# Mixer's end in a two-layer decoder trunk: one softmax scaling moved ahead of a recurrence level, and the first output product's parts taken in another order

## The chip, the core and the metric

One NeuronCore of a Trainium2 chip runs the whole step as one program. The engines have queues of their own and meet at semaphores: TensorE (PE; PEld is its weight load), VectorE (DVE), ScalarE (ACT), GpSimd (POOL), and SyncE (SP), which here only issues DMAs. The metric is the device time of one execution, in microseconds (us); smaller is better.

## The reference, cut to what matters

Two layers of a hybrid decoder run over 256 prompt tokens and 8 x 4 sampled tokens (288 columns, features on the 128 partitions). Only the mixer's end, where three branches meet in one output projection, is touched:

```python
def mixer_layer(x, pos, attn, hg_state, conv_prev, g, w_in_l, w_out_l, lb, norm_g, cw):
    h = rmsnorm(x, g) @ w_in_l
    ...
    a = attn(q, k, v)                                   # 512 features: softmax attention
    o_h, S = hgrn2_mixer(hq, hf, hi, hg, lb, norm_g, hg_state)   # 256: gated recurrence
    yc, conv_new = causal_dwconv(cc * ch, conv_prev, cw)
    o_c = cb * yc                                       # 256: gated convolution
    y = jnp.concatenate([a, o_h, o_c.astype(a.dtype)], axis=-1) @ w_out_l
    return x + y, k, v, S, conv_new
```

The recurrence's output is normalised per head (`rmsnorm(o, norm_g)`) and gated before it enters the product. After the mixer come a cross-attention over 256 memory tokens (memory keys and values of the prompt are computed, those of the samples are read from a cache), and a gated MLP.

## The kernel before, in words

`layer_schedule` (L142) writes one order of steps per layer by hand. Each step has a name, arguments and a letter: "A" or "D" says that PE fills a bank of PSUM for it and that ACT or DVE empties the bank; "op" is a step without a bank, of the engines that handle its name. Every engine walks the same list and does its own part of each step, so the list sets the order on PE, ACT, DVE and POOL at once. Banks are used in turn, eight of them.

The steps that matter, with the lines of the profile:

- `as`, `anorm`, `at`, `ao` of g = 0 to 3 (attention of the prompt): DVE subtracts the maximum, ACT takes the exponential (L1077, L1079), `anorm` scales the probabilities on DVE (L1932 to L1936), PE transposes them (`at`, L1451), ACT copies, PE multiplies by the values (`ao`, L1457 to L1461).
- `level(m)`: one level of the recurrence. PE (L1527) fills two banks, DVE places them with a mask (L1976), and `merge` (DVE, L1996 to L1998) scales for the next level. m = 64 is the last; `cross` (L1539) follows.
- `ss`, `st`, `so`, `sot`: attention of the samples (`so` is L1483 and L1486 on PE, its ACT part is L1103, `sot` is L1497 on PE).
- `mk`, `mv`: keys and values of the prompt's memory (L1409, L1417 on PE), each emptied by one ACT copy (L964). On POOL the step `mv` 1 (L856) waits for ACT's copy, stores mv to memory (issue at L813), and then builds a table `vexp` (L864).
- `ho` 0 and 1 (PE L1561 to L1571; DVE L2017, L2019): output of the recurrence, two heads in each half. `hn` 0 and 1: sum of squares over a head (PE L1574), ACT's guess of the root (L976, a function with a table of its own), three DVE operations that refine it (L1759 to L1764) and two that apply it (L2026, L2029). DVE takes half 0 wholly before half 1.
- `split_mixed` k: tile k of the eight input tiles of the output projection is split in a rounded high part (ACT, L1123) and the rest (DVE, L2034). Tiles 0 to 3 are attention, 4 and 5 the recurrence's halves, 6 and 7 the convolution. `MIXED_ORDER` (L78) is the order in which PE takes them in the first output block.
- `round` / `rest` "out" m: the same split of the weights of output block m (ACT L1168, DVE L1822). SP loads block m's weights when PE has finished with the buffer: blocks 2 and 3 when `mv` 1 is done on PE, block 4 when block 0 is, and so on.
- `out` m (PE L1288 to L1290, 24 matmuls a block), m = 0 to 7. After each of the first six stands `turn_cmem` m: PE transposes (L1427) a cached memory-key block that POOL has loaded into `rawk`, which has two halves. On POOL the step `turn_cmem` b issues the load of cached block b + 2 (L798, through `load_rawk(l, b + 10)`) and then one of values (L878). `turn_cmem` 2 on PE thus needs the load that POOL issues in its step `turn_cmem` 0, which stands behind `mv` 1 and the store of `hstate` in POOL's order:

```python
                elif step == "turn_cmem":
                    b = args[0]
                    if b < 6:
                        load_rawk(l, b + 10)
```

After the change `mv` 1 stands behind all of the second group of `split_mixed` and behind `round` "out" 1 in the list; PE's own order from `sot` to `out` 0 is `sot`, `mv` 0, `mv` 1, `hstate`, `out` 0 in both kernels.

Of the kernel before, what the change touches and what calls it, by code (L numbers as in the profile page):

```python
# [29 lines left out]
ACT = mybir.ActivationFunctionType  # L30
# [44 lines left out]
    return (n + 3) % SLOTS  # L75


MIXED_ORDER = [6, 7, 4, 5, 0, 1, 2, 3]  # L78
DOWN_K = [(0, 8), (8, 16), (16, 22)]


# [55 lines left out]
def par_col(r, l, k=0):  # L137

    return r[0] + l * r[1] + k


def layer_schedule(l):  # L142
# [5 lines left out]
    def a(who, step, *args):  # L148
        s.append((step, args, who))

    def level(m):
        a("D", "level", m, 0)
        a("D", "level", m, 1)
        a("op", "merge", m)
# [9 lines left out]
    def project(part, m):  # L164

        p = 2 * [c[0] for c in IN_CHUNKS].index(part) + m
        if 4 <= p + 2 < IN_PIECES:
            a("op", "rest", "in", p + 2, l)
        a("D", "in", part, m)
        if p == (2 if first else 1):  # L170
            a("D", "ssq", 0)
        if 4 <= p + 3 < IN_PIECES:
            a("op", "round", "in", p + 3, l)
# [96 lines left out]
    scores(3)  # L270
    project("hg", 1)
    a("A", "ao", 2)
    level(64)
    a("op", "anorm", 3)
    a("A", "ss", 0)
    turn_probs(3)
    a("A", "ss", 1)
# [9 lines left out]
        a("A", "turn_ke", t)  # L287
    a("A", "st", 1)
    a("op", "conv")
    a("A", "mk", 1)  # L290
    a("A", "so", 0)
    a("D", "ho", 0)
    a("D", "ho", 1)
    a("A", "so", 1)
    a("D", "hn", 0)
    a("D", "hn", 1)
    a("A", "sot")
    a("A", "mv", 0)
    for k in (6, 7, 4, 5):
        a("op", "split_mixed", k)  # L300
    a("A", "mv", 1)
    a("op", "round", "out", 0, l)
    a("op", "rest", "out", 0, l)
    for k in (0, 1, 2, 3):
        a("op", "split_mixed", k)
    a("op", "round", "out", 1, l)
    a("op", "rest", "out", 1, l)
    a("A", "hstate")
    for m in range(8):
# [109 lines left out]
class Banks:  # L419


    def __init__(self):
        self.steps = [(-1, *x) for x in PROLOGUE]
        for l in range(DEPTH):
            self.steps += [(l, *x) for x in layer_schedule(l)]
        self.steps += [(DEPTH, *x) for x in EPILOGUE]
        self.emptying_steps = emptied_order(self.steps)
        fills = [x for x in self.steps if x[3] != "op"]
        self.of = {x[:3]: n for n, x in enumerate(fills)}
        emptied = {}  # L430
        for who, steps in (("A", self.steps), ("D", self.emptying_steps)):
            own = [x for x in steps if x[3] == who]
            emptied.update({x[:3]: (who, n + 1) for n, x in enumerate(own)})
        self.before = [emptied[x[:3]] for x in fills]


def decoder_kernel(nc, a, out):
# [4 lines left out]
    with ExitStack() as ctx:  # L442
        def sb(name, *shape, dt=F32):
            return ctx.enter_context(nc.sbuf_tensor(name, list(shape), dt))
# [27 lines left out]
        mv = sb("mv", P, 2, 256)  # L472
# [4 lines left out]
        small = sb("small", P, 112)  # L477
# [109 lines left out]
        eps = small[:, 56:57]  # L587
# [74 lines left out]
        def wait_emptied(eng, l, step, *args):  # L662

            who, count = banks.before[banks.of[l, step, args]]
            eng.wait_ge(emptied[who], count)
# [285 lines left out]
        def _(act):  # L951
            ac = nc.scalar.activation
# [26 lines left out]
            def gained(l, stage, k):  # L979

                if stage == 3:
                    wait_emptied(act, l, "down", k)
                elif l == 0 and stage == 0:
                    wait_emptied(act, -1, "turn_x", k)
                else:
                    before = (l, "out") if stage else (l - 1, "down")
                    wait_emptied(act, *before, k)
                c = R_FINAL + k if stage == 3 else par_col((R_MIX, R_XATTN)[stage], l, k)
                if stage or l:
                    ac(XG[:, k], X[:, k], ACT.Identity, scale=par[:, c:c + 1]).then_inc(s["xg_tile"], 1)  # L990
                if stage == 0:
                    ac(xg_hi_mix[:, k], X[:, k], ACT.Identity, scale=par[:, c:c + 1]).then_inc(s["xg_hi"], 1)

            for l, step, args, who in banks.emptying_steps:
                if step == "turn_x" and who == "A":
                    take(l, step, args, X[:, args[0]], bank(l, step, *args)[:, 0:N]).then_inc(emptied["A"], 1)
                elif step == "hi_x":
                    if args[0] == 0:
                        wait_emptied(act, l, "par_mix")
                    gained(0, 0, args[0])  # L1000
                elif step == "root_first":
                    act.wait_ge(s["eps"], 1)
                    ac(small[:, 48:49], eps, ACT.Abs_reciprocal_sqrt)
# [111 lines left out]
                elif step == "split_mixed":  # L1115
                    k = args[0]
# [33 lines left out]
                elif step == "round":  # L1150
                    kind, i, l = args
# [101 lines left out]
        def _(pe):  # L1253
# [15 lines left out]
            def parts_of(l, kind, i):  # L1269

                count, _, lo, hi_part, width, _ = split_of(kind, i, l)
                pe.wait_ge(w_lo_dve, count)
                if kind in ("up", "down"):
                    pe.wait_ge(w_lo_pool, count - SPLIT_PIECES * (l + 1))
                return [w.rearrange("p (k c) -> p k c", c=width) for w in (hi_part, lo)]
# [39 lines left out]
            for l, step, args, who in banks.steps:  # L1315
# [259 lines left out]
                elif step == "out":  # L1575
                    m = args[0]
                    hi_w, lo_w = parts_of(l, "out", m)
                    for n, k in enumerate(MIXED_ORDER):
                        if m == 0:
# [101 lines left out]
        def _(dve):  # L1681
# [93 lines left out]
            for l, step, args, who in banks.emptying_steps:  # L1775
# [255 lines left out]
                elif step == "split_mixed":  # L2031
                    k = args[0]
                    dve.wait_ge(s["mixed_hi"], 8 * l + MIXED_ORDER.index(k) + 1)
                    v.tensor_tensor(mixed_lo[k], mixed[k], mixed_hi[:, k].bitcast(F32), ALU.subtract).then_inc(s["mixed_lo"], 1)  # L2034
# [100 lines left out]
```

## Time and profile before

| | |
|---|---|
| median of 3 runs | 882.81 us (879.73 to 885.25) |
| the profiled execution's own time | 884.58 us |
| its span, first to last instruction | 882.9 us (1.7 us lie outside) |
| PE busy | 840.1 us, 95% |
| DVE / ACT / POOL busy | 65% / 52% / 42% |
| mean granted clock of PE | 0.978 |

The mixer's end is at 121 to 191 us in the first layer and at 545 to 616 us in the second. A timeline row reads: start, duration, engine, line, operation, output <- input, partitions x elements, count, and in brackets how long the engine sat idle before it and what ended that.

### The profile page before, as it was taken

To read this page: it belongs to the slowest core of one execution; us is meant where nothing else is said; L and a number is where in the kernel's file an instruction comes from. 1 tells how busy PE (TensorE), PEld (TensorE's weight loads), DVE (VectorE), ACT (ScalarE), POOL (GpSimd) and SP (SyncE) were. 2 spreads that over 40 slices of the span, in tenths; PEclk is the share of its full clock that TensorE was granted. 3 is DMA by queue.
4 is the path that set the end of the run, shared out by engine and by line. 5 is a ranking of instruction groups with operands and counts; after the bars stand their busy time and mean duration, and the time that the engine had idled before them with its cause. 6 is when DMAs were issued, how large, how long until landed. Compare 5 with 4: busy or idle time off the path is not lost.

```text
span 882.9 us, 17206 instructions
## 1 busy us (share of the span) xinstructions
PE 840.1 (95%) x6422; PEld 783.3 (89%) x6422; DVE 575.8 (65%) x1249; ACT 456.2 (52%) x944; POOL 374.5 (42%) x344
## 2 busy tenths in 40 slices
PE   8999999997999999999999999989789899999996
PEld 6989877884998999999999987779579899999996
DVE  4787864754888777634366886476469887763342
ACT  5653543437657656534345355254665665654332
POOL 1422310524436555666742331043251665566552
PEclk9999999999999999999999999999989999999999
DMA  9765521668284656455658563148816465655532
GB/s 282 202 178 157 174 73 49 197 177 228 56 218 119 182 147 183 137 179 167 180 138 201 173 184 97 49 143 223 231 53 170 122 183 148 178 157 161 157 112 73
DMA packets 210110, 137.69 MB, mean 156 GB/s; under 512 B 23764, under 2 KB 202620, under 8 KB 210028
## 3 DMA queue, kind: packets, MB, share of 16 engines
q1 hardware_dynamic: 201024, 113.56, 45.5%
q0 software_dynamic: 8544, 22.85, 8.8%
q8 instruction: 52, 0.85, 0.4%
q10 hardware_dynamic: 459, 0.18, 0.1%
q14 instruction: 31, 0.25, 0.1%
HBM read 131.13 MB, written 5.44 MB: 155 GB/s over the span
## 4 chain that ended last, share of the span: by engine, by line
PE 72%; DVE 8%; DMA 6%; issue 6%; ACT 4%; POOL 1%; DVEq 1%; POOLq 1%; SPq 0%; ACTq 0%
PE banks L1288 19%; PE banks L1289 18%; PE banks L1290 18%; DMA ring<-in_w_up 4%; DVE ring_r L1822 3%; PE banks L1632 2%; PE banks L1283 2%; PE banks L1527 1%; PE banks L1427 1%; DVE phase L2092 1%; DMA ring<-in_w_in 1%; DVE XG_r L2077 1%; PE banks L1409 1%; PE banks L1417 1%; PE banks L1326 1%
## 5 line engine op out<-in xcount | busy, mean ns | idle before, releaser
L1290 PE MATMUL banks<-mix_r,ring_r 128*128 128x288 f32 x960 | 285.4, 297 | 0.0
L1290 PEld LDWEIGHTS banks<-mix_r,ring_r 128*128 128x128 f32 x960 | 183.6, 191 | 0.0
L1288 PE MATMUL banks<-mix_r,ring_r 128*128 128x288 f32 x480 | 149.3, 311 | 9.5 <-issue 6.3
L924 POOL TENSOR_TENSOR ring_r<-ring,keysT_r 128x512 fp32r<-128x512 f32 (+2 forms) x36 | 101.2, 2810 | 106.9 <-ACT keysT_r L1168 106.4
L1290 PE MATMUL banks<-phase_r,ring_r 128*128 128x288 f32 x416 | 122.5, 295 | 0.0
L924 POOL TENSOR_TENSOR ring_r<-ring,vals_r 128x512 fp32r<-128x512 f32 (+2 forms) x32 | 91.0, 2844 | 68.8 <-ACT vals_r L1168 68.3
L1168 ACT CAST ring_r<-ring 128x1024 fp32r<-128x1024 f32 x60 | 62.4, 1047 | 91.3 <-DMA ring<-in_w_in 60.9
L1288 PEld LDWEIGHTS banks<-mix_r,ring_r 128*128 128x128 f32 x480 | 91.9, 192 | 16.2 <-issue 11.0
L1289 PE MATMUL banks<-XG_r,ring_r 128*128 128x288 f32 x352 | 104.5, 297 | 0.0
L2092 DVE SCALAR_TENSOR_TENSOR phase<-banks,fpar,phase 128x255 f32<-128x255 f32 (+1 forms) x160 | 76.9, 481 | 42.2 <-ACT phase L1224 35.4
L1289 PE MATMUL banks<-XG_r,vals_r 128*128 128x288 f32 x320 | 95.8, 299 | 0.0
L1289 PE MATMUL banks<-XG_r,keysT_r 128*128 128x288 f32 x320 | 94.4, 295 | 0.0
L1822 DVE TENSOR_TENSOR ring_r<-ring,keysT_r 128x1536 fp32r<-128x1536 f32 (+1 forms) x36 | 56.4, 1568 | 52.2 <-ACT keysT_r L1168 52.2
L1822 DVE TENSOR_TENSOR ring_r<-ring,ring_r 128x1024 fp32r<-128x1024 f32 x60 | 74.3, 1242 | 17.2 <-ACT ring_r L1168 16.7
L1168 ACT CAST keysT_r<-ring 128x2048 fp32r<-128x2048 f32 (+1 forms) x36 | 66.9, 1859 | 28.3 <-DMA ring<-in_w_down 24.3
L1290 PEld LDWEIGHTS banks<-phase_r,ring_r 128*128 128x128 f32 x416 | 78.2, 188 | 0.0
L1222 ACT ACTIVATE phase<-banks,fpar 128x288 f32<-128x288 f32 x80 | 40.1, 501 | 72.3 <-PE banks L1290 72.3
L1822 DVE TENSOR_TENSOR ring_r<-ring,vals_r 128x1536 fp32r<-128x1536 f32 (+1 forms) x32 | 49.9, 1559 | 39.6 <-ACT vals_r L1168 39.6
L1288 PE MATMUL banks<-mix_r,vals_r 128*128 128x288 f32 x240 | 71.9, 300 | 3.9 <-DVE phase L2094 3.9
L1168 ACT CAST vals_r<-ring 128x2048 fp32r<-128x2048 f32 (+1 forms) x32 | 59.2, 1851 | 28.7 <-DMA ring<-in_w_down 25.7
L1288 PE MATMUL banks<-phase_r,keysT_r 128*128 128x288 f32 x240 | 71.9, 300 | 0.5 <-POOL ring_r L924 0.5
L1288 PE MATMUL banks<-mix_r,keysT_r 128*128 128x288 f32 x240 | 71.3, 297 | 0.9 <-DVE phase L2094 0.9
(315 smaller groups left out, 2069.2 us busy)
## 6 DMA issues: line engine op xcount, KB each, us to landing
ring<-in_w_up SPq DMA_DIRECT2D x88, 512.0 KB, 5.2
ring<-in_w_in SPq DMA_DIRECT2D x36, 512.0 KB, 4.3
ring<-in_w_down SPq DMA_DIRECT2D x16, 1024.0 KB, 5.2
ring<-in_w_down SPq DMA_DIRECT2D x8, 768.0 KB, 4.9
rawk<-in_cache_k POOLq DMA_DIRECT2D x32, 128.0 KB, 2.9
vals<-in_cache_v POOLq DMA_DIRECT2D x32, 128.0 KB, 2.6
ring<-in_w_in SPq DMA_DIRECT2D x16, 256.0 KB, 3.9
rawk<-in_cache_mem_k POOLq DMA_DIRECT2D x16, 256.0 KB, 5.2
```

The costliest lines, as they stand in the source:

```text
L924: g_.tensor_tensor(lo[:, cols], both[:, cols], hi_part[:, cols].bitcast(F32), ALU.subtract).then_inc(w_lo_pool, 1)
L1168: nc.scalar.copy(hi_part[:, 0:tiles * width], both[:, 0:tiles * width]).then_inc(w_hi, 1)
L1222: ac(yab[i % 2][ab], b_[:, 0:N], ACT.Identity, scale=fpar[:, 3 * l + 2, c:c + 1])
L1283: last = mm(out_[:, 0:N], w[:, k, cols], xg(l, stage, k), start=k == 0, stop=k == KT_D - 1)
L1288: mm(out_, hi_w, hi_x, start=start, stop=False)
L1289: mm(out_, hi_w, lo_x, start=False, stop=False)
L1290: return mm(out_, lo_w, hi_x, start=False, stop=stop)
L1326: mm(ps[:, 7, 0:N], sqr[:, 0:P], sqr[:], start=True, stop=True)
L1409: last = mm(o[:, 0:N_MEM], w[:, k], mg[:, k], start=k == 0, stop=k == KT_D - 1)
L1632: last = mm(o[:, 0:N], w[:, k, P * m:P * m + P], mix[:, k], start=k == 0, stop=k == 1)
L1822: v.tensor_tensor(lo[:, cols], both[:, cols], hi_part[:, cols].bitcast(F32), ALU.subtract).then_inc(w_lo_dve, 1)
L2092: v.scalar_tensor_tensor(out=y[:, d:SEQ], in0=b_[:, 0:SEQ - d], scalar=tap, in1=y[:, d:SEQ], op0=ALU.mult, op1=ALU.add)
```

## The change

`anorm` 3 goes ahead of `level(64)`. Among the last steps of the mixer `so` 0 and `ho` 0 go ahead of `mk` 1, and the splits of the two convolution tiles and the split of output block 0's weights go ahead of or around `ho` 1. A new ACT step `root_ready` evaluates the root function on one column, so that its table is loaded before `hn` 0. The recurrence's second half (tile 5) becomes the last of the eight tiles, and `mv` 1 goes behind the splits.

```diff
-MIXED_ORDER = [6, 7, 4, 5, 0, 1, 2, 3]
+MIXED_ORDER = [6, 7, 4, 0, 1, 2, 3, 5]
...
     a("A", "ao", 2)
+    a("op", "anorm", 3)
     level(64)
-    a("op", "anorm", 3)
     a("A", "ss", 0)
...
     a("op", "conv")
-    a("A", "mk", 1)
     a("A", "so", 0)
     a("D", "ho", 0)
+    for k in (6, 7):
+        a("op", "split_mixed", k)
+    a("A", "mk", 1)
+    a("op", "round", "out", 0, l)
     a("D", "ho", 1)
+    a("op", "rest", "out", 0, l)
     a("A", "so", 1)
+    a("op", "root_ready")
     a("D", "hn", 0)
     a("D", "hn", 1)
     a("A", "sot")
     a("A", "mv", 0)
-    for k in (6, 7, 4, 5):
-        a("op", "split_mixed", k)
-    a("A", "mv", 1)
-    a("op", "round", "out", 0, l)
-    a("op", "rest", "out", 0, l)
-    for k in (0, 1, 2, 3):
+    for k in (4, 0, 1, 2, 3, 5):
         a("op", "split_mixed", k)
     a("op", "round", "out", 1, l)
+    a("A", "mv", 1)
     a("op", "rest", "out", 1, l)
...
+                elif step == "root_ready":
+                    ac(small[:, 48:49], eps, ACT.Abs_reciprocal_sqrt)
```

## Rows read from the trace of the kernel before

**Rows 1.** Page, busy time by engine: us, share of the span, instructions.
```profile
PE 840.1 (95%) x6422; PEld 783.3 (89%) x6422; DVE 575.8 (65%) x1249; ACT 456.2 (52%) x944; POOL 374.5 (42%) x344
```

**Rows 2.** Waits of PE, whole span: us in total, times, longest us.
```profile
PE banks L1288 <- issue: 6.3, 3, 2.1
...
PE banks L1451 <- DVE phase L1936: 4.3, 2, 2.2
...
PE banks L1427 <- DMA rawk<-in_cache_mem_k: 1.1, 1, 1.1
```

**Rows 3.** Timeline of PE, first layer's mixer end.
```profile
125.97 0.85 PE L1451 MATMUL banks<-con,phase 128*128 128x128 f32 x6 [2.18 <-DVE phase L1936]
...
128.76 3.72 PE L1409 MATMUL banks<-XG,ring 128*128 128x256 f32 x16
...
144.52 1.64 PE L1486 MATMUL banks<-vals,phase 128*32 128x256 f32 x16
...
158.45 0.51 PE L1288 MATMUL banks<-mix_r,ring_r 128*128 128x288 f32 x1 [2.10 <-issue]
...
163.25 0.60 PE L1427 MATMUL banks<-con,rawk 128*128 128x128 f32 x4
...
170.51 0.60 PE L1427 MATMUL banks<-con,rawk 128*128 128x128 f32 x4
...
174.15 0.60 PE L1427 MATMUL banks<-con,rawk 128*128 128x128 f32 x4
```

**Rows 4.** Timeline of PE, second layer's mixer end.
```profile
553.15 4.36 PE L1409 MATMUL banks<-XG,ring 128*128 128x256 f32 x16
...
569.55 1.07 PE L1486 MATMUL banks<-vals,phase 128*32 128x256 f32 x16
570.55 1.24 PE L1574 MATMUL banks<-phase,con 128*128 128x288 f32 x4
...
579.06 0.69 PE L1548 MATMUL banks<-phase 128*64 128x64 f32 x16
```

**Rows 5.** Stretches: us, busy by engine, granted clock of PE, DMA share, GB/s.
```profile
551.00:552.00 1.00, 1.00 (x13) 0.17 (x5) 0.00 (x0) 0.52 (x2) 0.00 (x0) 0.53 0.00 0
...
158.50:160.00 1.50, 1.50 (x7) 1.50 (x8) 1.33 (x4) 1.43 (x4) 0.19 (x1) 0.51 0.57 178
```

**Rows 6.** Chain that ended last, 579 to 596 us: start, us, what.
```profile
579.84 0.80 POOL out L813
...
583.06 5.05 POOL XG L864 x4
...
589.35 5.69 DMA rawk<-in_cache_mem_k
...
595.17 0.63 PE banks L1427 x4
```

**Rows 7.** Timelines of ACT (first line) and POOL, first layer.
```profile
155.78 0.37 ACT L964 COPY mv<-banks 128x256 f32<-128x256 f32 x1 [0.42 <-PE banks L1417]
166.03 0.73 POOL L798 DMA_DIRECT2D rawk<-in_cache_mem_k  x1
```

**Rows 8.** Landing of the load of rawk that POOL issues at 166.03.
```profile
DMA to landing us min/median/max: 4.0/4.0/4.0
```

**Rows 9.** Timeline of DVE: ahead of level 64 (first layer), end of root chain (second).
```profile
122.33 0.99 DVE L1976 COPY_PREDICATED phase<-mask,banks 128x256 f32<-128x256 int32 x2 [1.45 <-PE banks L1527]
...
578.26 0.52 DVE L2029 SCALAR_TENSOR_TENSOR phase<-phase,par 128x288 f32<-128x288 f32 x1
```

**Rows 10.** Timeline of ACT, root, mv 1 and weight splits, second layer.
```profile
571.38 1.28 ACT L976 ACT_TABLE_LOAD   x1 [0.16 <-PE banks L1574]
572.68 0.50 ACT L976 ACTIVATE vv<-banks,small 128x288 f32<-128x288 f32 x1
...
579.17 0.37 ACT L964 COPY mv<-banks 128x256 f32<-128x256 f32 x1
...
584.98 1.05 ACT L1168 CAST ring_r<-ring 128x1024 fp32r<-128x1024 f32 x1 [1.36 <-DMA ring<-in_w_out]
```

## The prediction

> **What bounds the kernel now.** I read the page first: PE is busy for 95% of the span, DVE for 65% and POOL for 42% [rows 1], so only what shortens PE's own stream or its idle time can count. The list of PE's waits comes next [rows 2]. It has what the change aims at: 4.3 us in two waits of the last `at` for DVE's scaled probabilities, one per layer, and 6.3 us in three waits ahead of an output block, two of them in these stretches. The timeline of PE places them: 2.18 us ahead of L1451 and 2.10 ahead of `out` 0 in the first layer [rows 3]; both come again in the second, 2.1 us each by the longest and the total in the list. The reader should also see how long equal work takes: `so` 1 (L1486) has 1.64 us in the first layer and 1.07 in the second, `mk` 0 (L1409) has 3.72 and 4.36 [rows 3, 4]. The stretches say why: at 551 us and at 158.5 us the granted clock is 0.53 and 0.51, that is 1.2 GHz and not 2.4, the first after a wait of 2.1 us and thin matmuls, the second after a wait of 2.1 us [rows 5]. The first output block pays for this: from its start to the next transposes go 163.25 - 158.45 = 4.80 us, where a later block and its transposes take 174.15 - 170.51 = 3.64 together [rows 3]. With some 0.4 of these for the transposes, a block takes 3.2, and the low clock cost 1.6.
>
> The chain of waits tells a second thing. In the second layer the end was not set by PE here but by POOL: store of mv at 579.84, the table at 583.06 for 5.05 us, the issue of the third cached key block at 589.35, 5.69 us to landing, and PE's `turn_cmem` 2 at 595.17 [rows 6]. PE had idled 1.1 us for it [rows 2]. In the first layer the same load was issued at 166.03, 10.25 us after ACT began to copy mv (155.78) [rows 7]. It needed 4.0 us [rows 8], landed at 170.0, and PE was there at 170.51 [rows 3]: a slack of only 0.5 us.
>
> **Part 1, `anorm` 3 ahead of `level(64)`.** DVE stood idle for 1.45 us ahead of L1976 [rows 9], and the four scalings fit in it almost to the end; the level is then late by 0.1 at most, which nothing near waits for (`cross` needs its merge only behind `at`, `ss` 1). PE reaches L1451 as it did and goes on at once: -2.18 and -2.1 us of idle, -4.3 in all [rows 2, 3]. If the cover were gone, the level would be late by the scalings' 1.4 us, still under the 2.1 saved.
>
> **Part 2, PE's low clock.** With that idle gone and `mk` 1's dense matmuls between the thin ones of `ho` 0 and `ho` 1, I take the dips ahead of the root as gone. In the first layer this is worth 1.64 - 1.07 = 0.57 up to the end of `so` 1 [rows 3, 4]. In the second the slow stretch holds `mk` 0, 0.64 longer than in the first layer, and the thin matmuls ahead of it, also at half the clock [rows 5]: 1.6 in all, taken from the first block's. Lower bound: nothing, if the clock falls all the same.
>
> **Part 3, the root's table.** `root_ready` adds one column (0.2 us) and takes the load of 1.28 us from behind `hn` 0's matmuls to behind `so` 1's copy. In the second layer the load stood there already, only 0.16 us after its releaser [rows 10]. I cost it at +0.04. The page "ScalarE: Activation LUTs" of the Trainium skill, under "What ACT_TABLE_LOAD costs", puts a switch of tables at about 2.66 us with its drain. Here the root follows its load of 1.28 by 0.02 us, so the trace shows no such drain; by the page some 1.4 us more would be moved, and as the place is the same for both, the sum would stay as it is.
>
> **Part 4, the tiles and the splits.** Let S be the end of `so` 1 on PE (570.55 in the second layer, no dip near) [rows 4]. The root chain ends on DVE at 578.26 + 0.52 = S + 8.2 [rows 9], PE's `hstate` at 579.06 + 0.6 = S + 9.1 [rows 4]. Before, the weights of block 0 were split only afterwards, and PE stood for 2.1 us more, until S + 11.2. Now they are ready, tiles 6 and 7 too; the rests of the six tiles follow the chain on DVE; at 0.4 each, an estimate from their size beside L2029's 0.52 (128 x 288 too), the last, tile 5's, is there at S + 10.6, and PE wants it at S + 9.1 + 7 x 0.4 = S + 11.9. So `out` 0 starts at S + 9.1 without a wait: 2.1 us earlier, and with no idle before it at full clock, 1.6 us shorter. Block 0 ends at S + 12.3, block 1 at S + 16. Block 2's weights are loaded when `mv` 1 is done, as before (PE's order there is the same): at S + 14.4 ACT has them (584.98) [rows 10], and with ACT's and DVE's split block 2 starts at about S + 16.7. PE is at `turn_cmem` 2 at S + 20.0. Before it went on there at S + 24.6 (595.17) in the second layer [rows 6].
>
> **Part 5, what the move of `mv` 1 costs.** This is the step I give most weight. ACT's copy of mv now waits for tile 5's rounding, as before, and also for `round` "out" 1, 1.05 us like the other casts of L1168 [rows 10]. It starts at 579.17 + 1.05 = S + 9.7 instead of S + 8.6. POOL waits for it, and behind it in POOL's queue stand the store, the table, the store of `hstate` and the load for `turn_cmem` 2, 10.2 us in both layers [rows 6, 7]: issue at S + 19.9, landing 4.0 to 5.7 later [rows 6, 8], S + 23.9 to S + 25.6. PE stands there for 4 to 6 us, where nothing else is in its way. The 2.1 + 1.6 us of part 4 are given back whole. The next load (values between, 1.4 us later, 6 us to land at the most) is there at S + 27.3, before PE wants it at S + 28. Bounds beyond this: none for less than 4.0 (no row has it), 5.7 the most.
>
> After such a wait I expect the low clock once more, now on block 3: 1.6 us by the row of block 0 [rows 3], 3.2 if it lasts twice as long, nothing if it holds, as it did after the wait of 2.18 us in the first layer. I take 1.6. The page "TensorE: Matmul & The Clock Gate" of the Trainium skill, under "HAM oscillation", describes just this, PE idling for a DMA and restarting cold each time. It speaks against the change, the trace agrees at 158 us, and by it the term is the same 1.6.
>
> **The sum,** against the profiled execution's own time, 884.58 (span 882.9 and 1.7 outside it). First layer: S moves from 144.52 + 1.64 less 0.07 of overlap = 146.09 to 146.09 - 2.18 - 0.57 = 143.34. `turn_cmem` 2 then comes at 167.2 to 168.9 instead of 170.51: 1.6 to 3.3 us gained, middle 2.4, less 1.6 for the clock: 0.8. Second layer: S from 570.55 to 570.55 - 2.10 - 1.6 = 566.85, `turn_cmem` 2 at 590.8 to 592.4 instead of 595.17: 2.7 to 4.4 gained, middle 3.6, less 1.6: 2.0. Behind that point each block follows at its own pace, and the later loads hang on PE's steps, so the gain reaches the end. Sum -2.8 of 884.58, 881.8; the profiled execution lies 1.8 above the median shown, so 880.0.
>
> **The rivals.**
> Main case (A), POOL holds `turn_cmem` 2: 880.0, from 875.5 (landing 4.0, clock holds) to 885 (landing 5.7, one dip stays, clock low for longer). Chance 0.72.
> (B) POOL's work doesn't bind: were the load there in time, PE would pass `turn_cmem` 2 at S + 20.0, at 163.3 and 586.9, 7.2 and 8.3 us earlier, with no cold block 3. That makes 884.6 - 15.5 - 1.8 = 867.3. The 10.2 us of POOL in both layers speak against it; that parts of it are waits for no shown cause (2.3 to 2.6 us between store and table) leave it a chance. 0.08.
> (C) The other side: PE's clock. If the thin matmuls bring the dips as before (no 0.57, no 1.6), the landing is 5.7, and the long wait costs two low stretches, 3.2 a layer, the layers come to 170.51 - 169.6 - 3.2 = -2.3 and 595.17 - 594.2 - 3.2 = -2.2: 4.5 us slower, 887.3. It decides from 2.5 us of loss a layer after the wait. Chance 0.14; to pass 1% it would need a landing of 8 us as well.
> (D) The gain is there up to the output blocks and is lost behind them, to the loads of the MLP's weights in the cross-attention: 882.8. They are released by PE's own steps, which speaks against it. 0.06.
>
> **How the numbers follow.** What a measurement of this kernel can tell from no change is about 1%, 8.8 us (its three runs span 5.5). The predicted time is that of A, 880.0. The range reaches from 873.5, a little under A's low end by half the runs' spread, to 887, which holds most of C; B lies outside. Faster by over 1% (under 874.0) is B and a tail of A: 0.13. Slower by over 1% (over 891.6): a tail of C, 0.04. Within 1%: 0.83.
>
> **What would show it.** Right: no wait of PE ahead of L1451 and of `out` 0 in either layer; one of 4 to 6 us ahead of `turn_cmem` 2 in both, with the DMA of `rawk` as releaser; the chain through POOL's store, table and load in both layers; the copy of mv behind the rounding of block 1's weights; a granted clock near 0.5 on block 3. Wrong: if that wait is under 2 us, B holds; if PE still waits for L1451, part 1 failed; if `out` 0 waits for tiles, part 4 did; if the time leaves the range with these rows in place, the clock's terms were mis-sized.

## The result: 879.96 us, 0.65% less than before, and the profile after

| | before | after |
|---|---|---|
| median | 885.45 us (20 runs, 878.93 to 895.04) | 879.96 us (20 runs, 875.05 to 884.34) |
| ratio to before, 95% interval | | 0.9935 (0.9915 to 0.9956) |
| the profiled execution's own time, span | 884.58, 882.9 us | 877.62, 875.8 us |

The absolute time came out as predicted, 880.0. Part of that is luck: the prediction stood on a median of 882.81 for the kernel before, and 20 runs put it at 885.45. As a difference it forecast 2.8 us, and 5.5 came, nearly twice as much.

First PE's waits in the profile after, in the columns of [rows 2]. The wait for L1451's operands (L1454 now) is not in the list any more, the load of `rawk` leads it, and the one "issue" left lies elsewhere.

```profile
PE banks L1430 <- DMA rawk<-in_cache_mem_k: 4.8, 2, 2.5
...
PE banks L1291 <- DVE ring_r L1825: 3.4, 3, 1.3
PE banks L1291 <- issue: 2.4, 1, 2.4
```

The timeline of PE after, first layer (the first seven lines) and second (the last two), beside [rows 3, 4]:

```profile
123.76 1.11 PE L1530 MATMUL banks<-phase 64*128 64x64 f32 x16
...
126.36 0.88 PE L1454 MATMUL banks<-con,phase 128*128 128x128 f32 x6
...
146.13 1.24 PE L1577 MATMUL banks<-phase,con 128*128 128x288 f32 x4
...
154.65 0.69 PE L1551 MATMUL banks<-phase 128*64 128x64 f32 x16
...
163.93 0.37 PE L1291 MATMUL banks<-mix_r,ring_r 128*128 128x288 f32 x1 [1.16 <-DVE ring_r L1825]
...
169.69 0.63 PE L1430 MATMUL banks<-con,rawk 128*128 128x128 f32 x4 [2.36 <-DMA rawk<-in_cache_mem_k]
173.33 0.60 PE L1430 MATMUL banks<-con,rawk 128*128 128x128 f32 x4
...
589.65 0.63 PE L1430 MATMUL banks<-con,rawk 128*128 128x128 f32 x4 [2.46 <-DMA rawk<-in_cache_mem_k]
...
594.82 0.60 PE L1430 MATMUL banks<-con,rawk 128*128 128x128 f32 x4
```

The last `at` starts 2.60 us behind `level(64)` (126.36 - 123.76) without a wait, where 4.85 us lay between before. The thin `hn` matmuls take 1.24 us in the first layer too, `hstate` is followed by `out` 0 at once. Then PE stands twice: 1.16 us for the weights of block 2 and 2.36 us for `rawk`. Block 3 with its transposes takes 173.33 - 169.69 = 3.64 us in the first layer, the full-clock pace of [rows 3], and 594.82 - 589.65 = 5.17 in the second. The stretches, in the columns of [rows 5], show the granted clock in the two: 1.00 and 0.50, that is 2.4 and 1.2 GHz.

```profile
170.00:174.00 4.00, 4.00 (x33) 4.00 (x32) 0.50 (x2) 0.68 (x2) 1.41 (x2) 1.00 1.10 299
...
592.00:594.00 2.00, 2.00 (x10) 2.00 (x10) 0.00 (x0) 0.00 (x0) 0.03 (x1) 0.50 1.17 287
```

The timeline of ACT after, first layer: the root's table behind `so` 1, and mv's copy now behind the cast of block 1's weights.

```profile
146.82 1.28 ACT L1003 ACT_TABLE_LOAD   x1
148.12 0.20 ACT L1003 ACTIVATE small<-small 128x1 f32<-128x1 f32 x1
148.23 0.48 ACT L977 ACTIVATE vv<-banks,small 128x288 f32<-128x288 f32 x1
...
154.93 1.04 ACT L1171 CAST ring_r<-ring 128x1024 fp32r<-128x1024 f32 x1
155.88 0.36 ACT L965 COPY mv<-banks 128x256 f32<-128x256 f32 x1
```

The timeline of POOL after, first layer, answering to [rows 6, 7], and the landing of the store issued at 156.54 (first) and of the load of `rawk` issued at 165.87 (second):

```profile
156.54 0.79 POOL L814 DMA_DIRECT2D out<-mv  x1 [28.19 <-ACT phase L965]
159.65 5.03 POOL L865 TENSOR_TENSOR XG<-phase,con 32x512 f32<-32x512 f32 x4 [2.32 <-issue]
164.63 1.27 POOL L814 DMA_DIRECT2D out<-phase  x2
165.87 0.73 POOL L799 DMA_DIRECT2D rawk<-in_cache_mem_k  x1
```
```profile
out<-mv POOLq DMA_DIRECT2D x1, 256.0 KB, 2.9
```
```profile
DMA to landing us min/median/max: 3.7/3.7/3.7
```

S is again the end of `so` 1 on PE, the start of `hn` 0 (146.13 and 566.16 after). The table is worked out from starts in PE's timelines, first / second layer, in us. "Front" is from `level(64)` to S; the other columns count from S, and what stands behind S is called the tail; `hstate_s`, behind block 6, stands for the end of the mixer. The last four rows are kernels of the experiments below.

| kernel | front | `hstate` | `out` 0 | `turn_cmem` 2 | `hstate_s` |
|---|---|---|---|---|---|
| before | 24.97 / 25.90 | 9.58 / 8.51 | 12.36 / 11.30 | 24.42 / 24.62 | 39.29 / 39.24 |
| after | 22.37 / 22.37 | 8.52 / 8.51 | 9.13 / 9.13 | 23.56 / 23.49 | 38.16 / 39.63 |
| scaling moved alone | 23.63 / 22.18 | 10.28 / 8.51 | 13.06 / 11.30 | 25.10 / 23.95 | 40.56 / 38.58 |
| tail alone | 26.16 / 26.28 | 8.52 / 8.51 | 9.13 / 9.13 | 24.10 / 23.29 | 40.24 / 39.42 |
| after, `mk` 1 back | 23.35 / 23.80 | 10.61 / 10.05 | 11.22 / 10.66 | 25.72 / 24.74 | 40.32 / 39.75 |
| after, no drain | 22.38 / 22.37 | 8.51 / 8.51 | 9.12 / 9.13 | 20.62 / 20.78 | 35.43 / 39.25 |

Read down the first and the last column: of the 6.9 us that the two layers lose (64.26 + 65.14 before, 60.53 + 62.00 after, from `level(64)` to `hstate_s`), 6.1 are in the front and 0.7 in the tail, although the tail starts its output product 2.2 to 3.2 us earlier. The span fell by 7.1, but the rest of it is not level: in the profiled execution of the changed kernel `level(64)` of the first layer came 2.64 us later than before (123.76 for 121.12), behind steps that the change does not touch, and what follows the second layer's `hstate_s` was 3.06 us shorter. Over all traces here that last part takes 268.5 to 273.1 us, whatever the tail's order. So single stretches outside the mixer's end say nothing of the change, and a difference of 2 or 3 us between two spans can come from there.

### The profile page after: what moved, and what is told of

Its sections match the earlier page's. It is cut to its first block, busy times and chain, and to the rows that moved or that the text cites. A ratio compares the mean times of both kernels' runs of the same rounds, so it can differ in the third digit from the quotient of the medians.

```text
span 875.8 us, 17208 instructions
## 1 busy us (share of the span) xinstructions
PE 837.8 (96%) x6422; PEld 780.6 (89%) x6422; DVE 574.4 (66%) x1249; ACT 455.6 (52%) x946; POOL 374.6 (43%) x344
## 4 chain that ended last, share of the span: by engine, by line
PE 68%; issue 8%; DVE 8%; DMA 6%; ACT 3%; POOL 3%; DVEq 1%; POOLq 1%; SPq 0%; ACTq 0%
PE banks L1291 19%; PE banks L1293 18%; PE banks L1292 18%; DMA ring<-in_w_up 4%; DVE ring_r L1825 2%; PE banks L1635 2%; PE banks L1286 2%; PE banks L1530 1%; PE banks L1430 1%; POOL XG L865 1%; DMA ring<-in_w_in 1%; DVE phase L2095 1%; PE banks L1329 1%; POOL XG L853 1%; DMA rawk<-in_cache_mem_k 1%
## 5 line engine op out<-in xcount | busy, mean ns | idle before, releaser
L1825 DVE TENSOR_TENSOR ring_r<-ring,ring_r 128x1024 fp32r<-128x1024 f32 x60 | 74.2, 1241 | 16.9 <-ACT ring_r L1171 16.4
```

What stands on the lines that cost most here:

```text
L1825: v.tensor_tensor(lo[:, cols], both[:, cols], hi_part[:, cols].bitcast(F32), ALU.subtract).then_inc(w_lo_dve, 1)
```

## The experiments

**The two halves of the change, each alone.** First the scaling moved in the kernel before:

```diff
     a("A", "ao", 2)
+    a("op", "anorm", 3)
     level(64)
-    a("op", "anorm", 3)
```

> Only the scaling of the last probabilities moves ahead of the last level; all else as before. Theory (POOL's chain hangs on S, the end of so 1, and so on the start of the whole tail): PE loses its 2.1 us wait ahead of L1451 in both layers, and everything behind it, POOL's chain too, comes 2.1 us earlier, so 3.5 to 6 us are gained, a ratio of 0.993 to 0.996, about as much as the whole change; the wait ahead of out 0 stays at 2.1 us and turn_cmem 2 waits 0 to 1.5 us for rawk. Rival (the tail's reordering carries the gain): at most 2 us here, ratio 0.998 or more.

Measured: 0.9943 (0.9906 to 0.9979), 878.78 us. Then the changed kernel with these two lines turned round again, all of the tail's edits kept:

> The changed kernel with the scaling put back behind the last level: the tail's reordering alone. Theory: out 0 starts 2 us earlier and is not slow, but POOL's load for turn_cmem 2 comes 1 us later than before, so PE waits 2 to 4 us there; the total is within 2 us of before, ratio 0.998 to 1.002. Rival (the reordering carries the gain by itself): 3 us or more faster, ratio 0.996 or less.

Measured: 1.0049 (1.0020 to 1.0078), 886.17 us. The scaling alone gives what the whole change gives, and the rival falls: the reordered tail gains nothing by itself. It is even 0.5% slower, outside my 0.998 to 1.002. Its rows show the mechanism of the loss: `out` 0 at S + 9.13, and PE's waits

```profile
PE banks L1430 <- DMA rawk<-in_cache_mem_k: 5.0, 2, 2.8
```

with block 3 slow behind the wait in both layers (5.19 and 5.17 us), and the clock low behind L1454's wait in both (fronts of 26.2). The product of the two ratios is 0.9992, the whole change 0.9935; the intervals leave room for most of that gap. That the rest is how often the clock falls is a guess that no run here shows; the next run bears on it.

**The place of `mk` 1.** Undone alone in the changed kernel:

```diff
+    a("A", "mk", 1)
     a("A", "so", 0)
     a("D", "ho", 0)
     for k in (6, 7):
         a("op", "split_mixed", k)
-    a("A", "mk", 1)
     a("op", "round", "out", 0, l)
```

> The changed kernel with mk 1 back ahead of so 0 and ho 0, so that the thin matmuls of ho 0 and ho 1 stand together again. Theory (the mixture with dense matmuls holds PE's clock): the granted clock falls to 0.5 after the two in one or both layers, so 1 and the root's matmuls are slower by up to 1.6 us; the time is 0 to 2 us above the changed kernel's, ratio to before 0.993 to 0.996. Rival (the place of mk 1 doesn't matter): no low clock there, ratio 0.9935.

Measured: 0.9937 (0.9907 to 0.9966), 880.31 us. The stretches of this run, in the columns of [rows 5], behind `ho` 0 and `ho` 1 in the two layers:

```profile
144.00:148.00 4.00, 4.00 (x18) 2.61 (x11) 1.35 (x4) 2.35 (x4) 0.00 (x0) 0.50 0.00 0
...
568.00:572.00 4.00, 4.00 (x21) 2.51 (x14) 1.24 (x3) 2.35 (x4) 0.00 (x0) 0.50 0.00 0
```

The clock falls in both, and not in the kernel after: there the stretch from 144 to 148 us has 1.00. Over all profiles of this study, `hstate` came at S + 8.5 in each of the 18 layers in which dense matmuls stand between the two halves, and later (9.6 to 10.6) in 4 of 10 in which they don't. In five of these ten the clock had already fallen behind the wait ahead of the last `at`, and there it held behind `ho`; of the other five it fell in four. So in these traces the dense matmuls between the halves go with a clock that holds. In the profiled execution it costs time: counted from `level(64)`, `turn_cmem` 2 comes 3.1 and 2.7 us later than in the kernel after (23.35 + 25.72 and 23.80 + 24.74, for 45.93 and 45.86), and `hstate_s` 3.1 and 1.6. The medians don't show it: 880.31 of 8 executions beside 879.96 of 20, and both readings of the expectation allowed 0.9937. Why not stays open.

**POOL's table of 5 us, moved behind the loads.** The table's four heads go one behind each load of `turn_cmem` 1 to 4:

```diff
                 elif (step, args) == ("mv", (1,)):
                     ...
-                    pool.drain()
-                    for h in range(4):
-                        last = g_.tensor_tensor(
-                            vexp[:, h], ...
...
                     pool.dma_start(vals[:, b], src).then_inc(vals_in, 16)
+                    if 1 <= b <= 4:
+                        h = b - 1
+                        wait_emptied(pool, l, "turn_hi", 2)
+                        pool.wait_ge(con_in, 32)
+                        pool.drain()
+                        last = g_.tensor_tensor(
+                            vexp[:, h], ...
```

> The changed kernel with POOL's table of 5 us cut in its four heads, one behind each of the loads of turn_cmem 1 to 4, so that the load for turn_cmem 2 is issued some 5 us earlier. Theory (POOL's queue takes back the gain): the wait of 2.4 us ahead of turn_cmem 2 is gone in both layers, block 2's weights become the only wait (about 1 us), and block 3 is not slow; 5 to 7 us faster than the changed kernel, a ratio to before of 0.985 to 0.988. Rival (the load's landing is bound by DMA traffic, not by its issue): the wait stays above 1.5 us, ratio 0.992 to 0.995.

Measured: 1.0077 (1.0043 to 1.0111), 890.08 us, 10 us slower than the changed kernel. Neither theory had this. PE passed `turn_cmem` 2 at S + 20.2 and 20.9, as I wanted, but then it waited for a later load of `rawk` (7.4 us in two waits) and, at `hstate_s`, for the table:

```profile
PE banks L1558 <- POOL XG L877: 5.1, 2, 3.4
```

POOL's timeline shows why, a gap that I had taken for a fixed cost; below it the landing of the load of values issued at 163.09:

```profile
163.09 0.72 POOL L871 DMA_DIRECT2D vals<-in_cache_mem_v  x1
169.33 1.03 POOL L877 TENSOR_TENSOR XG<-phase,con 32x512 f32<-32x512 f32 x1 [5.52 <-issue]
```
```profile
DMA to landing us min/median/max: 5.8/5.8/5.8
```

163.09 + 5.8 = 168.9: the head starts 0.4 us after the load has landed. The next two heads follow loads issued at 171.06 and 177.27, with landings of 4.2 and 5.0, and start at 175.53 and 182.45, 0.2 to 0.3 behind. The theory formed from it is that the drain ahead of an arithmetic instruction of POOL waits for POOL's own DMAs. In the kernel after it fits too: the store issued at 156.54 lands 2.9 later, at 159.4, and the table starts at 159.65.

**The same without the drain**, one execution:

> The run with the table's four heads behind the loads of turn_cmem 1 to 4, now without POOL's drain ahead of each. Theory (the drain waits for POOL's own DMAs to land): the gaps of 2.8 to 5.5 us between a load's issue and the next head are gone (under 0.5 us), and the wait of 3.4 us for the table too. Rival (the gap is a cost of going from DMA issues to an arithmetic instruction): the gaps stay.

Measured: 875.12 us, one execution, so its time alone says little; the trace says more. The gap is gone, the only edit against the run before being the drain:

```profile
162.32 0.72 POOL L871 DMA_DIRECT2D vals<-in_cache_mem_v  x1
163.06 1.06 POOL L876 TENSOR_TENSOR XG<-phase,con 32x512 f32<-32x512 f32 x1
```

So the "issue" ahead of the table, 2.41 us between 580.65 and 583.06 in [rows 6], is the landing of a store (issued at 579.84, 3.0 us to land), and not a cost of the table. Here PE's waits moved to the weights' splits: 6.1 us in eight waits for DVE's L1826, where the changed kernel has 3.4 in three.

**The table ahead of the store.** If the theory holds, the drain costs nothing where no DMA of POOL's is in flight:

```diff
-                    wait_emptied(pool, l, "mv", 1)
-                    store(mem_v_prompt[l, 0].rearrange("(t p) h d -> p t (h d)", p=P), mv[:])
-
+                    pe_done(pool, l, "mv", 1)
                     wait_emptied(pool, l, "turn_hi", 2)
                     ...
                     last.then_inc(s["vexp_ready"], 1)
+                    wait_emptied(pool, l, "mv", 1)
+                    store(mem_v_prompt[l, 0].rearrange("(t p) h d -> p t (h d)", p=P), mv[:])
```

> The changed kernel with POOL's table ahead of the store of mv, released by PE's end of mv 1 and not by ACT's copy. Theory after the runs before (POOL's step ahead of the table waits until POOL's own DMAs have landed, and the table holds back the load for turn_cmem 2): the 2.1 to 2.3 us between store and table are gone, the load is issued at about S + 15.7 in place of S + 19.7, PE waits less than 0.5 us at turn_cmem 2 and block 3 is not slow; 4 to 7 us faster than the changed kernel, ratio to before 0.986 to 0.989. Rival (the load's landing is set by DMA traffic): the wait stays above 1.5 us and the ratio at 0.992 or more.

Measured: 0.9890 (0.9856 to 0.9923), 876.13 us. The wait for `rawk` is gone and block 3 is fast, the gain is at the low end of what I expected. The trace also has the drain itself, which the timelines leave out: the two of the kernel before, ahead of the table (first line), and the two of this run (second), count, shortest/median/longest in ns, and when:

```profile
L862 POOLq DRAIN  x2: 3065/3135/3205, 156.5 to 579.9; - x2
```
```profile
L861 POOLq DRAIN  x2: 46/46/46, 154.5 to 570.8; - x2
```

The reason for the small gain is on DVE. This is the timeline of POOL (first line) and of DVE's six splits ahead of `out` 0:

```profile
154.60 4.69 POOL L863 TENSOR_TENSOR XG<-phase,con 32x512 f32<-32x512 f32 x4 [26.67 <-PE banks L1420]
```
```profile
153.93 5.68 DVE L2037 TENSOR_TENSOR phase_r<-phase,mix_r 128x288 fp32r<-128x288 f32 x6
```

The same six take 2.29 us where POOL's table is not running (the run without the drain, below). PE waited for them in block 0, which took from S + 9.13 to 14.33, 5.2 us and not 3.3. The same edit in the kernel before:

> The same move in the kernel before. There PE reaches turn_cmem 2 later, with a wait of 0 to 1.1 us. Theory: only that wait goes, 0 to 1.5 us faster, ratio 0.998 to 1.001, much less than the same edit brings in the changed kernel. Rival (the edit helps by itself, whatever the tail's order): 4 us or more in both kernels, ratio 0.995 or less.

Measured: 1.0033 (1.0004 to 1.0062), 888.09 us: no gain at all, a small loss outside my 1.001. The rival, a gain in both, falls too. The table now stood beside the splits and weights that `out` 0 waits for; PE's wait ahead of `out` 0 was 4.3 us in place of 2.10 [rows 3], and DVE's timeline has 3.25 us for four splits and 2.06 for a weight split that takes 1.2 alone:

```profile
580.24 3.25 DVE L2034 TENSOR_TENSOR phase_r<-phase,mix_r 128x288 fp32r<-128x288 f32 x4
583.41 2.06 DVE L1822 TENSOR_TENSOR ring_r<-ring,ring_r 128x1024 fp32r<-128x1024 f32 x1
```

The Trainium skill, "SBUF — State Buffer", section "SBUF: two separate sides", says that GpSimd and VectorE share a pair of ports as an exclusive lock, taken for a whole instruction, by a VectorE instruction with two SBUF inputs too. These rows agree: subtractions of two SBUF tensors that overlap the table grew by 1.7 to 3.4 us in all. Instruction by instruction, two of the six splits above run before the table and take 0.45 us each, and the other four take 1.29 to 1.30, one beside each instruction of the table. The term was not in my prediction; the lines of the kernel after that it bears on are the splits of block 2's weights in the two layers:

```profile
161.74 2.04 DVE L1825 TENSOR_TENSOR ring_r<-ring,ring_r 128x1024 fp32r<-128x1024 f32 x1 [1.99 <-ACT ring_r L1171]
...
582.41 1.22 DVE L1825 TENSOR_TENSOR ring_r<-ring,ring_r 128x1024 fp32r<-128x1024 f32 x1 [1.76 <-ACT ring_r L1171]
```

The first began 0.08 us behind an instruction of the table and took 2.04. The second began at 582.41, 0.10 us ahead of one, and took 1.22; there the table's instruction took 2.02 us in place of 1.03.

**mv's copy earlier**, ahead of the split of tile 5:

```diff
-    for k in (4, 0, 1, 2, 3, 5):
+    for k in (4, 0, 1, 2, 3):
         a("op", "split_mixed", k)
-    a("op", "round", "out", 1, l)
     a("A", "mv", 1)
+    a("op", "split_mixed", 5)
+    a("op", "round", "out", 1, l)
```

> The changed kernel with ACT's copy of mv 1 ahead of the split of tile 5 and of the weights of block 1. Theory: POOL starts 1.2 us earlier, the wait ahead of turn_cmem 2 falls from 2.4 to about 1.2 us in both layers, out 0 is not delayed; 2 to 2.5 us faster than the changed kernel, ratio to before 0.990 to 0.992. Rival (the place of mv 1 doesn't matter): ratio 0.9935 and a wait of 2.4 us.

Measured: 0.9915 (0.9878 to 0.9953), 876.56 us. The ratio is in the expected band, but its interval holds the changed kernel's 0.9935, and its trace has PE at `turn_cmem` 2 at S + 24.0 and 22.7, with 5.8 us of waits for `rawk`, more than the changed kernel's 4.8. In the first layer the load was issued 0.7 us earlier and not 1.2 (S + 19.1), and landed after 4.8 us, where it took 3.7 in the changed kernel. Inconclusive: the spread of the landing is as large as the step.

**The drain taken out of the changed kernel**, nothing else:

```diff
                     wait_emptied(pool, l, "turn_hi", 2)
                     pool.wait_ge(con_in, 32)
-                    pool.drain()
                     for h in range(4):
```

> The changed kernel without POOL's drain ahead of the table, all else in place. Theory (POOL's drain waits for the landing of the store of mv, and the table otherwise only holds the load back): the 2.1 to 2.3 us between store and table are gone, the load for turn_cmem 2 is issued at S + 17.5, PE's wait there falls from 2.4 us to under 0.6, block 3 keeps the full clock, out 0 starts at S + 9.1 without the slow splits of the table-first run; 3.5 to 6 us faster than the changed kernel, ratio to before 0.986 to 0.990. Rival (traffic sets the landing): wait above 1.5 us, ratio 0.992 or more.

Measured: 0.9822 (0.9779 to 0.9864), 871.32 us: better than both kernels by more than the intervals, and more than the 0.986 that I expected at best. POOL and DVE in the first layer:

```profile
155.39 0.79 POOL L814 DMA_DIRECT2D out<-mv  x1 [28.19 <-ACT phase L964]
156.20 4.44 POOL L864 TENSOR_TENSOR XG<-phase,con 32x512 f32<-32x512 f32 x4
160.59 1.27 POOL L814 DMA_DIRECT2D out<-phase  x2
161.82 0.73 POOL L799 DMA_DIRECT2D rawk<-in_cache_mem_k  x1
```
```profile
153.08 2.29 DVE L2036 TENSOR_TENSOR phase_r<-phase,mix_r 128x288 fp32r<-128x288 f32 x6
```

The table follows the store by 0.02 us, the splits are over before it starts, and PE is at `turn_cmem` 2 at S + 20.6 and 20.8, within 0.8 us of the S + 20.0 of rival B. The load was issued at S + 16.8 and 16.9. Of the wait for `rawk` 1.1 us are left in two waits, 0.3 at `turn_cmem` 2 of the first layer and 0.8 at `turn_cmem` 3 of the second; the weights lead PE's list (the counts are over the whole span):

```profile
PE banks L1290 <- DVE ring_r L1824: 5.5, 6, 1.6
...
PE banks L1429 <- DMA rawk<-in_cache_mem_k: 1.1, 2, 0.8
```

The account doesn't reach the whole gain. From `level(64)` to `hstate_s` the two layers take 119.4 us here and 122.5 in the kernel after: 3.1 us, where the medians differ by 8.6. The mean granted clock of these 6 executions is 0.9885, that of the changed kernel's 20 is 0.9806, so PE also spent less time at 1.2 GHz elsewhere; no run here shows why.

With mv's copy early on top:

> The run without the drain, with ACT's copy of mv 1 also ahead of the split of tile 5. Theory: the load is issued 1.2 us earlier still, at S + 16.3, but PE no longer waits for it, so nothing more is gained; and the table, earlier by 1.2 us, runs beside DVE's splits of tile 5 and of block 1's weights, which then take longer. Within 1 us of the run without the drain, ratio 0.986 to 0.991. Rival (POOL still holds PE): 2 us faster than that run.

Measured: 0.9855 (0.9809 to 0.9901), 872.90 us. Nothing more is gained, as expected; the 1.6 us between the two medians are within the intervals. But the load hardly moved, S + 16.7 and not 16.3: the table started earlier and took 5.41 us in place of 4.44 in the first layer, where a weight split beside it took 2.06. So this run doesn't test whether POOL still holds PE. And the drain taken out of the kernel before:

> The kernel before without POOL's drain ahead of the table, the edit that gave the changed kernel its best time (ratio 0.982). Theory (in the order of before, PE comes late to turn_cmem 2 and hardly waits for POOL): the load is issued 2.3 us earlier, a wait of at most 1.1 us in one layer goes; against it the table, 2.3 us earlier too, runs beside DVE's splits ahead of out 0 and lengthens them, up to 1 us in each layer; ratio 0.997 to 1.003, so that the tail's reordering is worth what lies between, 1.5% less what the moved scaling gives. Rival (the drain costs by itself): the same 8 us as in the changed kernel, ratio 0.991 or less.

Measured: 0.9982 (0.9951 to 1.0014), 884.91 us. The same one line is worth 1.1% behind the changed order (0.9822 against 0.9935) and nothing that can be told behind the old one, where the earlier table again fell beside DVE's four splits and took them from 1.56 us to

```profile
160.01 4.95 DVE L2033 TENSOR_TENSOR phase_r<-phase,mix_r 128x288 fp32r<-128x288 f32 x4
```

**The root's early table**, taken out, one execution:

> The changed kernel without root_ready. Theory: the table of the root is loaded right behind the copy of so 1 anyway, or 0.2 us later behind the root's first matmuls, whichever comes last; the root chain ends within 0.3 us of where it did relative to S (S + 8.1), and the time is that of the changed kernel, 875 to 885. Rival (the early load pays): the guess comes 1 us later, and with it POOL's load and turn_cmem 2, 2 us in all.

Measured: 880.06 us. The timeline of ACT, first layer, S = 145.72:

```profile
146.55 1.28 ACT L976 ACT_TABLE_LOAD   x1 [0.16 <-PE banks L1576]
147.84 0.50 ACT L976 ACTIVATE vv<-banks,small 128x288 f32<-128x288 f32 x1
```

The guess starts at S + 2.12 without `root_ready` and at 148.23 - 146.13 = S + 2.10 with it. The guess is not earlier for it, and by this row it gains nothing.

## Why the prediction was right

**Part 1** held: no wait ahead of the last `at`, DVE's part of `level(64)` late by some 0.2 us where I had put 0.1 at most, and nothing waited for it. The run of this edit alone carries the result.

**Part 2** held in the profile. The front is 22.37 us in both layers, 2.60 and 3.53 less than before, for 2.75 (2.18 + 0.57) and 3.7 (2.10 + 1.6) in the sum. Two causes were mixed in it, and the runs part them. The wait of 2.1 us ahead of L1451 went with a low clock behind it in 7 of the 8 layers that had it (fronts of 25.9 to 26.3; the first layer of before is the eighth). `mk` 1 between the halves goes with a clock that holds behind `ho`, but the medians show no time for it.

**Part 3**: nothing gained and nothing lost, as costed.

**Part 4** held up to block 1: `out` 0 at S + 9.13, its transposes at S + 12.4, the next at S + 16.0. Block 2 was to start at S + 16.7 and started at S + 17.8 (163.93) and S + 17.6 (583.78). In the first layer the reason is that DVE's split of its weights took 2.04 us beside POOL's table. In the second the split took 1.22; there ACT's cast of the weights began only at 581.33 = S + 15.2, behind their load, where I had S + 14.4. Missed: the contention of the two engines, though the kernel before shows it as well: its weight splits at 160.10 and 583.49 us, beside the table, took 1.82 and 1.71 us where the next ones took 1.21.

**Part 5**, the decisive one, was right in mechanism and place. The load was issued at S + 19.74 and 19.60 (19.9 forecast), PE went on at S + 23.56 and 23.49. The size was off: the landing took 3.7 and 3.8 us, below the 4.0 that I had put down as the least (the middle of my bounds was 4.85), and with block 2 late PE stood 2.4 us and not 4 to 6. My test "under 2 us, B holds" was near to deciding wrongly on that.

**The clock on block 3** came in one layer of two: 5.17 against 3.64 us, 1.53 for 1.6 forecast, in the second; nothing in the first. The forecast stood on the row at 158 us, where PE had waited 2.10 us for split weights and not for a DMA; over all traces with a wait of over 2 us for `rawk` the clock fell in 5 layers of 10.

**The sum.** From `level(64)` to `hstate_s` the first layer gained 3.7 us for 0.8 forecast and the second 3.1 for 2.0. In the first, the landing makes 1.1 of the difference of 2.9, the clock that held 1.6, the issue 0.2; in the second the landing's 1.05 is nearly all of it. So the term that was mis-sized is the wait at `turn_cmem` 2 with what follows it. Counted from the start of the execution, S of the first layer came at 146.13 and not at the 143.34 of my sum, since `level(64)` itself was 2.64 us late there; the part behind the second layer's `hstate_s`, 3.06 us shorter, made up for it. I had forecast neither, and that the two cancel is luck. Rival D, a loss behind the mixer, leaves no sign in the traces, but they vary too much there to exclude 1 or 2 us of it; the kernel with the scaling moved alone keeps its gain to the end. Rival C's cases occurred one by one (a low clock behind L1454 in the tail-alone run, behind `ho` with `mk` 1 back), not in the changed kernel. Rival B was near to what POOL's queue was worth: with the drain gone, PE passed `turn_cmem` 2 6.4 and 7.4 us earlier than before, counted from `level(64)`, where B had 7.2 and 8.3. Of these 13.8 us 10.0 were left at `hstate_s`, the rest going to waits for weights. That the ratio came to 0.982, the same as B's 867.3 of 882.81, is partly luck. And its one doubt, that the 2.3 us between store and table are "waits for no shown cause", was the point on which all of it hung.

## What to carry to other kernels

When steps of one hand-written list are reordered, follow each moved step on every queue that walks the list: here the reordering brought PE to `turn_cmem` 0 3.6 to 4.7 us earlier per layer (S + 12.4 for S + 16.0 and 17.2) and gave nearly all of it back, mostly to a load that stood behind a store, a drain and a table in POOL's queue. The gap called "issue" ahead of the table was a wait with a cause; where you find one, lay the landings of the same engine's DMAs beside it before pricing it as fixed. And an order that puts an idle engine's work earlier can put it beside work that it slows: look at what the neighbour does in that stretch.

## What the runs showed of the hardware that was not expected

- POOL's drain ahead of the table waits for the DMAs that POOL itself has issued: the gaps above, 2.3 to 5.5 us, ended 0.2 to 0.4 us after the landing of the last one (five cases). Over all traces it took 2.8 to 3.2 us in the 14 layers in which the store of mv had just been issued, and 0.05 us in the 4 in which nothing of POOL's was in flight. Without the drain the gap is 0.02 us.
- Subtractions on DVE of two SBUF tensors slow down beside POOL's multiplications, one instruction of the one for one of the other: a split from 0.45 to 1.30 us, and so 6 splits from 2.29 to 5.68, 4 splits from 1.56 to 3.25 and 4.95, a weight split from 1.22 to 2.06.
- A wait of PE of 2.1 us ahead of thin matmuls was followed by 1.2 GHz in 7 of 8 layers, those of 2.2 to 3.5 us for `rawk` ahead of the dense matmuls of block 3 in 5 of 10 (5.2 us a block with its transposes, and not 3.64), over the changed kernel and four variants of it.
